# The last expert step's down projection reordered by columns in a decoder layer with 32 experts

## The reference, cut to what matters

```python
def expert_block(args):                 # xb: the tokens of one expert, e: its number
    xb, e = args
    return (jax.nn.silu(xb @ w1[e]) * (xb @ w3[e])) @ w2[e]
...
out = out.at[row_tok].add(yr * row_w[:, None])     # weighted, back to the token's row
...
x = x + hier_moe(rms_norm(x, norm_moe), ...)
return rms_norm(x, final_norm)
```

## Time and profile before

| | us |
|---|---|
| median of 3 runs | 675.01 (674.87 to 675.44) |
| the profiled execution | 675.29 |
| its span | 673.5 |
| PE busy | 511.5 |
| DVE, ACT, POOL busy | 204.5, 145.5, 14.9 |
| DMA moved | 244.21 MB, mean 363 GB/s |

### The profile page before, as it was taken

How to read it: one execution, slowest core, us unless ns; L and a number is a source line. 1 busy time by engine, 2 the same in 40 slices (tenths; PEclk the granted TensorE clock), 3 DMA queues, 4 the chain that set the end, 5 groups by cost and what they waited for, 6 DMA issues and landing times.

```text
span 673.5 us, 8778 instructions
## 1 busy us (share of the span) xinstructions
PE 511.5 (76%) x3804; PEld 322.7 (48%) x3804; DVE 204.5 (30%) x378; ACT 145.5 (22%) x252; POOL 14.9 (2%) x31
## 2 busy tenths in 40 slices
PE   8999999999999997967744846774374667348475
PEld 7999998999999742422311411231141123114121
DVE  4899565588857431100000100000010000001002
ACT  5764545354635411000000000000000000000002
POOL 1200010001001000000000000000000000000001
PEclk9999999999999988997857988786797778679788
DMA  8999236908679999999999999999999999999994
GB/s 290 386 325 326 90 126 198 372 4 300 224 279 387 417 366 431 427 427 427 430 424 431 424 431 424 432 423 429 428 427 429 425 430 427 428 426 429 425 410 168
DMA packets 46041, 244.21 MB, mean 363 GB/s; under 512 B 5968, under 2 KB 15664, under 8 KB 34224
## 3 DMA queue, kind: packets, MB, share of 16 engines
q1 hardware_dynamic: 46000, 243.62, 89.4%
HBM read 242.53 MB, written 4.22 MB: 366 GB/s over the span
## 4 chain that ended last, share of the span: by engine, by line
PE 53%; DMA 44%; DVE 1%; ACT 1%; issue 0%; SPq 0%; POOL 0%; POOLq 0%
PE ps L713 16%; DMA slots_late<-in_w 13%; PE ps L1077 11%; DMA slots_own<-in_w 9%; DMA attn_data<-in_w 7%; PE ps L736 7%; PE ps L1082 6%; DMA slot_spare<-in_w 5%; DMA slot_last<-in_w 5%; DMA slot_mixed<-in_w 4%; PE ps L691 1%; DMA slots_own<-in_w_in 1%; PE ps L837 1%; PE ps L866 1%; PE ps L1187 1%; PE ps L951 1%
## 5 line engine op out<-in xcount | busy, mean ns | idle before, releaser
L1077 PE MATMUL ps<-slots_late,x_sb 128*32 128x512 f32 x320 | 88.2, 697 | 36.6 <-DMA slots_late<-in_w 14.7
L1077 PE MATMUL ps<-slot_spare,x_sb 128*32 128x512 f32 x128 | 60.8, 675 | 13.7 <-DMA attn_data<-in_w 13.7
L1077 PE MATMUL ps<-attn_data,x_sb 128*32 128x512 f32 x160 | 61.9, 701 | 10.7 <-DMA slots_own<-in_w 10.7
L1820 DVE TENSOR_TENSOR slot_extra<-ps,slot_extra 128x512 f32<-128x512 f32 x8 | 5.5, 692 | 212.2 <-ACT slot_extra L1443 212.2
L439 DVE TENSOR_TENSOR w_low<-slots_own,w_high 128x2048 fp32r<-128x2048 f32 (+1 forms) x32 | 64.7, 2021 | 16.8 <-ACT w_high L1251 16.5
L1440 ACT ACTIVATE slot_extra<-ps 128x256 f32<-128x256 f32 x8 | 3.1, 384 | 299.7 <-PE ps L1145 299.7
L1077 PE MATMUL ps<-slots_own,x_sb 128*32 128x512 f32 x240 | 56.7, 664 | 8.8 <-DMA slot_last<-in_w 3.6
L1082 PE MATMUL ps<-slots_own,slot_extra 128*32 128x512 f32 x192 | 50.1, 723 | 16.1 <-DMA slots_late<-in_w 8.0
L1082 PE MATMUL ps<-attn_data,slot_extra 128*32 128x512 f32 x112 | 46.4, 749 | 16.4 <-DMA slots_own<-in_w 16.4
L1251 ACT ACTIVATE w_high<-slots_own 128x2048 fp32r<-128x2048 f32 (+1 forms) x32 | 54.3, 1697 | 19.5 <-PE ps L736 10.8
L713 PE MATMUL ps<-h_high,w_high 128*128 128x256 f32 x224 | 55.4, 288 | 0.0
(11 more groups left out here) (262 smaller groups left out, 868.5 us busy)
## 6 DMA issues: line engine op xcount, KB each, us to landing
slots_own<-in_w SPq DMA_DIRECT2D x27, 2048.0 KB, 31.4
slots_late<-in_w SPq DMA_DIRECT2D x23, 2048.0 KB, 35.0
attn_data<-in_w SPq DMA_DIRECT2D x16, 2048.0 KB, 34.3
slot_last<-in_w SPq DMA_DIRECT2D x9, 2048.0 KB, 35.9
slots_own<-in_w_in SPq DMA_DIRECT2D x8, 2048.0 KB, 10.9
slot_spare<-in_w SPq DMA_DIRECT2D x8, 2048.0 KB, 34.7
slot_mixed<-in_w SPq DMA_DIRECT2D x7, 2048.0 KB, 34.7
slots_own<-in_w_out SPq DMA_DIRECT2D x2, 2048.0 KB, 9.7
```

Of the source, the lines that this page charges most:

```text
L1077: return pe.matmul(ps[SLOTS * e:SLOTS * e + SLOTS, 4 + matrix, :], xeT[:, k, SLOTS * e:SLOTS * e + SLOTS], w, start=(k == 0), stop=(k == K ...
L1820: dve.tensor_tensor(act_sb, ps[:, 5, :].rearrange("p (q f) -> p f q", f=FC), silu_sb.rearrange("p (f q) -> p f q", f=FC), ALU.mult).then_i ...
```

## The change

The diff replaces the tail of the last step. Loads: unit 10's slot now gets depths 2 and 3 of the left columns as two transfers of 1 MB, unit 11's slot depth 2 of the right columns (1 MB) and depth 3 of the right columns in two transfers of 0.5 MB (256 columns each). PE: the right half is computed as two quarters of 256 columns in banks 5 and 6; after the left half is complete, PE waits for ACT's copy of it and does both left scatters, and only then turns to depths 2 and 3 of the right half. DVE copies the right half in two quarters, and the right scatters are done by quarters.

```diff
--- before.py
+++ after.py
@@ -61,6 +61,9 @@
 SLOT = 4096
 SLICE = SLOT // SHARE
 MOE_CHUNKS = 12
+TAIL_LOADS = {10: [(0, 512, 2, 0, 0), (2048, 512, 3, 0, None)],
+              11: [(0, 512, 2, 512, 1), (2048, 256, 3, 512, 2), (3072, 256, 3, 768, None)]}
+TAIL_BANKS = [(4, 0, 512), (5, 512, 256), (6, 768, 256)]
 UNROLL = 2
 TURNS = STEPS // UNROLL
 TURN_CHUNKS = UNROLL * MOE_CHUNKS
@@ -351,7 +354,9 @@
         summed, again_done, fsq, frstd_set, out_written = (
             sem("summed"), sem("again_done"), sem("fsq"), sem("frstd_set"), sem("out_written"))
         left_weighted, left_set = sem("left_weighted"), sem("left_set")
-        var_left_set, last_half_in = sem("var_left_set"), sem("last_half_in")
+        var_left_set = sem("var_left_set")
+        tail_in = [sem(f"tail_in{i}") for i in range(3)]
+        y_mid_done, y_mid_copied = sem("y_mid_done"), sem("y_mid_copied")
         out_set = [sem(f"out_set{t}") for t in range(TT)]
         dve_step, pool_step = sem("dve_step"), sem("pool_step")
         sel_made, moved = sem("sel_made"), sem("moved")
@@ -536,14 +541,12 @@
                     e = step * SHARE + 2 * (j - 8)
                     sp.dma_start(ring[s].rearrange("p (e n) -> p e n", e=2),
                                  expert_weights[2][:, e:e + 2, 0:2 * SLICE]).then_inc(slot_in[s], 16)
-                elif step == STEPS - 1 and j == 10:
-                    load_slice(2, step * SHARE, 2, SLICE, ring[s], slot_in[s])
-                elif step == STEPS - 1 and j == 11:
-                    for c in range(2):
-                        n = 3 * SLICE + 512 * c
-                        sp.dma_start(ring[s].rearrange("p (e c n) -> p c e n", e=SHARE, c=2)[:, c],
-                                     expert_weights[2][:, step * SHARE:(step + 1) * SHARE,
-                                                       n:n + 512]).then_inc(last_half_in if c else slot_in[s], 16)
+                elif step == STEPS - 1 and j in (10, 11):
+                    for at, width, f, c0, signal in TAIL_LOADS[j]:
+                        signal = slot_in[s] if signal is None else tail_in[signal]
+                        src = expert_weights[2][:, step * SHARE:(step + 1) * SHARE, f * D + c0:f * D + c0 + width]
+                        sp.dma_start(ring[s][:, at:at + SHARE * width].rearrange("p (e n) -> p e n", e=SHARE),
+                                     src).then_inc(signal, 16)
                 else:
                     load_unit(j // SHARE, step * SHARE + j % SHARE, s, slot_in[s])
 
@@ -1152,24 +1155,59 @@
                 m.then_inc(actT_done, 1)
                 pe.wait_ge(actT_copied, it + 2)
                 if slices_out:
+
+                    def tail_matmul(piece, f, e, w):
+
+                        bank, _, width = TAIL_BANKS[piece]
+                        return pe.matmul(ps[SLOTS * e:SLOTS * e + SLOTS, bank, 0:width],
+                                         actT[:, f, SLOTS * e:SLOTS * e + SLOTS], w,
+                                         start=(f == 0), stop=(f == FC - 1), skip_group_check=True)
+
+                    def tail_load(j, i):
+
+                        at, width, f, c0, _ = TAIL_LOADS[j][i]
+                        s = unit_landed((STEPS - 1) * MOE_CHUNKS + j)[0]
+                        w = ring[s][:, at:at + SHARE * width].rearrange("p (e n) -> p e n", e=SHARE)
+                        for piece, (_, first, n) in enumerate(TAIL_BANKS):
+                            if c0 <= first < c0 + width:
+                                for e in range(SHARE):
+                                    m = tail_matmul(piece, f, e, w[:, e, first - c0:first - c0 + n])
+                        return m
+
+                    def scatter(t, piece):
+
+                        bank, c0, width = TAIL_BANKS[piece]
+                        return pe.matmul(ps[:, 2 * t + c0 // 512, c0 % 512:c0 % 512 + width],
+                                         selwT[:, t * P:(t + 1) * P], y_sb[:, c0:c0 + width],
+                                         start=False, stop=True, skip_group_check=True)
+
                     w = [unit(8 + i).rearrange("p (e f n) -> p e f n", e=2, f=2) for i in range(2)]
                     for f in range(2):
-                        for c in range(2):
+                        for piece, (_, c0, width) in enumerate(TAIL_BANKS):
                             for e in range(SHARE):
-                                m = down_matmul(c, f, e, w[e // 2][:, e % 2, f, 512 * c:512 * c + 512])
+                                m = tail_matmul(piece, f, e, w[e // 2][:, e % 2, f, c0:c0 + width])
                     m.then_inc(chunk_used, 2)
-                    w = unit(10).rearrange("p (e n) -> p e n", e=SHARE)
-                    for c in range(2):
-                        for e in range(SHARE):
-                            m = down_matmul(c, 2, e, w[:, e, 512 * c:512 * c + 512])
-                    m.then_inc(chunk_used, 1)
-                    w = unit(11).rearrange("p (e n) -> p e n", e=SHARE)
-                    for c in range(2):
-                        if c:
-                            pe.wait_ge(last_half_in, 16)
-                        for e in range(SHARE):
-                            m = down_matmul(c, 3, e, w[:, e, 512 * c:512 * c + 512])
-                        m.then_inc((y_left_done, chunk_used)[c], 1)
+                    pe.wait_ge(tail_in[0], 16)
+                    tail_load(10, 0)
+                    unit(10)
+                    tail_load(10, 1).then_inc(y_left_done, 1)
+                    pe.wait_ge(selwT_copied, it + 2)
+                    pe.wait_ge(y_copied_a, it + 2)
+                    for t in range(TT):
+                        scatter(t, 0).then_inc(summed, 1)
+                    pe.wait_ge(tail_in[1], 16)
+                    tail_load(11, 0).then_inc(chunk_used, 1)
+                    pe.wait_ge(tail_in[2], 16)
+                    tail_load(11, 1).then_inc(y_mid_done, 1)
+                    unit(11)
+                    tail_load(11, 2).then_inc(chunk_used, 1)
+                    pe.wait_ge(y_mid_copied, 1)
+                    scatter(0, 1)
+                    pe.wait_ge(y_copied_v, it + 2)
+                    scatter(0, 2).then_inc(summed, 1)
+                    scatter(1, 1)
+                    scatter(1, 2).then_inc(added, 1)
+                    return
                 else:
                     w = [unit(8 + e).rearrange("p (f n) -> p f n", f=FC) for e in range(SHARE)]
                     for c in range(2):
@@ -1186,8 +1224,6 @@
                     for t in range(TT):
                         m = pe.matmul(ps[:, 2 * t + c, :], selwT[:, t * P:(t + 1) * P], y_sb[:, 512 * c:512 * c + 512],
                                       start=False, stop=True, skip_group_check=True)
-                        if slices_out and c + t < 2:
-                            m.then_inc(summed, 1)
                 m.then_inc(added, 1)
 
             for signal in (added, actT_done, selwT_done):
@@ -1786,7 +1822,7 @@
 
             slots = const[:, K_SLOT:K_SLOT + SLOTS].unsqueeze(1).unsqueeze(1).to_broadcast([P, TT, SHARE, SLOTS])
 
-            def expert_step(it, experts, r, first=False):
+            def expert_step(it, experts, r, first=False, last=False):
                 if first:
                     dve.wait_ge(rank_done, 1)
                 else:
@@ -1821,6 +1857,13 @@
                                   silu_sb.rearrange("p (f q) -> p f q", f=FC), ALU.mult).then_inc(act_set, 1)
                 dve.wait_ge(actT_done, it + 2)
                 dve.tensor_copy(actT.rearrange("p f s -> p (f s)"), ps[:, 6, :]).then_inc(actT_copied, 1)
+                if last:
+                    dve.wait_ge(y_mid_done, 1)
+                    dve.wait_ge(added, it + 1)
+                    dve.tensor_copy(y_sb[:, 512:768], ps[:, 5, 0:256]).then_inc(y_mid_copied, 1)
+                    dve.wait_ge(chunk_used, it * MOE_CHUNKS + MOE_CHUNKS)
+                    dve.tensor_copy(y_sb[:, 768:1024], ps[:, 6, 0:256]).then_inc(y_copied_v, 1)
+                    return
                 dve.wait_ge(chunk_used, it * MOE_CHUNKS + MOE_CHUNKS)
                 dve.wait_ge(added, it + 1)
                 dve.tensor_copy(y_sb[:, 512:1024], ps[:, 5, :]).then_inc(y_copied_v, 1)
@@ -1829,7 +1872,7 @@
                 dve.sem_inc(signal, 1)
             dve.sem_inc(xe_copied, 2)
             for it in range(STEPS):
-                expert_step(it, slice(it * SHARE, it * SHARE + SHARE), 0, first=(it == 0))
+                expert_step(it, slice(it * SHARE, it * SHARE + SHARE), 0, first=(it == 0), last=(it == STEPS - 1))
             dve.wait_ge(most_set, 1)
             fullest = dve.value_load(most_i[0:1, 0:1], min_val=0, max_val=T)
             with dve.If(fullest > SLOTS):
```

## The result

The changed kernel takes 676.21 us, the kernel before 674.83 (medians of 22 runs each): ratio 1.0022, 95% interval 1.0015 to 1.0029. It is slower by about 0.2%; that is small, but the interval leaves out no change. (A ratio here is not the quotient of the two medians; the two differ by up to 0.001.) The forecast was 675.0 with 674.1 to 676.0, so the median lies outside. The profiled execution took 675.88 with a span of 674.1.

What follows compares the result with a forecast made beforehand. The present end was read as hanging on the last load's landing, with 1.6 us of PE slack; after the change PE would set it. 675.01 - 0.5 (earlier squares) + 0.5 (mean clock) = 675.0 us, range 674.1 to 676.0.

Steps and rivals of the forecast that it cites:

- both right squares start 0.5 us earlier: ACT's squares at the end: start 0.5 us earlier, still 0.86 apart, with POOL, DVE and SP following unchanged.
- the sum: Whole kernel: median 675.01, less 0.5 for earlier squares, plus 0.5 for the mean clock, gives 675.0 us.
- PE and not the last load set the end: Last quarter of the right half: its data land at 662.6, 1.3 us early, so PE's work sets the end.
- The sum of PE's terms: PE from 654.53: 1.85 us of waiting goes; 0.9 ACT's copy, 0.3 DVE's, 0.25 switches and starts come in.
- Short passes: PE's 256-column passes in the right half: 0.215 us each, bound 0.25.
- ACT's copy: Between PE's left passes and left scatters: PE idle 0.9 us, to 660.6, waiting for the copy.
- the cut loads: Last weight transfers, cut into smaller pieces: last landing at 662.6, 663.0 at most.
- the gains' landing: Load of the gains behind the weights: lands near 664.0, before DVE wants it.
- DVE's weightings: DVE's two left weightings run from about 665.6 to 667.1, covered by 0.4 us before the inverse root at 667.5.
- The slower rival, late loads: Last 0.5 MB: cut transfers land late; whole gain gone at 664.4, 678.2 us if landing at 667.6; chance 8%.
- The mean-clock term: PE's restart at half clock in the last step: mean clock starts the down matmuls 0.55 us later, longest 1.05.

Runs made afterwards that it cites:

- a_nobranch_warm: Changed kernel without PE's fallback branch, plus 14 matmuls on old data in the wait ahead of the last step's w3 matmuls: 674.28 us, ratio 0.9994.
- a_same: The changed kernel again, unchanged, as a control: ratio 1.0013 against the kernel before.
- a_nobranch: Changed kernel with PE's fallback for fuller experts (its last branch and body) left out: 673.76 us, ratio 0.9987 against the kernel before.
- a_else: Changed kernel with PE's last step put into both arms of its branch, so the jump comes near 612 us: 674.21 us, ratio 0.9994.
- a_mid: Changed kernel with PE's branch moved into the wait ahead of the last step's w3 matmuls, near 628 us: 674.62 us, ratio 1.0001.
- a_later: Changed kernel with one PE wait ahead of its last branch, until its last scatter is done: ratio 1.0014 against the kernel before.
- b_nobranch: Kernel before with PE's fallback for fuller experts (its last branch and body) left out: 674.35 us, ratio 0.9989.
- b_else: Kernel before with PE's last step put into both arms of its branch: 676.90 us, ratio 1.0032, 7 launches only.
- b_mid: Kernel before with PE's branch moved into the wait ahead of the last step's w3 matmuls: 675.76 us, ratio 1.0006.
- a_else_leftlate: As a_else, with the two left scatters moved behind the last quarter's down matmuls: 675.20 us, ratio 1.0007 against the kernel before.
- before: The kernel before the change, unaltered: 674.83 us, median of 22 runs.
- b_late: Kernel before with one PE wait ahead of its last branch, until the second left scatter is done: 676.29 us, ratio 1.0016.
- b_later: Kernel before with one PE wait ahead of its last branch, until PE's last scatter is done: ratio 1.0024.

## Why the prediction was wrong

**The step that failed** is the sentence that both right squares start 0.5 us earlier "and POOL, DVE and SP follow them unchanged". They did, to the issue of the output (1.07 us earlier in the profile); the DMA engines behind them did not. The last piece landed 4.6 us after its issue in place of 2.6, and the output as a whole took 1.65 us more, over three times the gain of 0.5. Put into the sum, 675.0 + 1.65 is 676.65, against the 676.21 measured. The output was costed as a fixed tail, and the one instruction packet at its edge was not looked for, though the trace of before had it, over just as the output began. What is late next was asked only up to the last compute instruction.

**Right, point by point.** PE and not the last load set the end: the chain and `a_nobranch_warm` show it. The sum of PE's terms: from the first down matmul to the right square 11.28 us, and 11.28 again in the profiles of `a_same`, `a_nobranch`, `a_else`, `a_mid` and `a_later`; the forecast was 0.5 below 11.76. Short passes cost 0.215, ACT's copy left PE idle for 0.81, the cut loads landed on time (the last at 662.47, forecast 662.6), the gains' landing at 663.7 (664.0), and DVE's weightings stayed covered. The slower rival, late loads, did not happen; that the time came out on its side is luck, as it was output and not weights that came late.

**The clock.** The mean-clock term was 0.5 us. In this profile the mean clock of the 6 us after the restart was 0.75, higher than in any of the six of the earlier trace rows:

```profile
641.90:647.90 6.00, 5.99 (x44) 1.84 (x48) 0.00 (x0) 0.00 (x0) 0.00 (x0) 0.75 1.00 416
```

In `a_nobranch` the rise came 5.3 us after the restart in place of 3.0 here, and the down matmuls began 13.18 us after it in place of 12.03: half the difference, as the step said. The Trainium skill's rule that this transition moves from run to run (TensorE: Matmul & The Clock Gate, Part 1) agrees with these rises. They lie further apart, 2.3 us, than the 500 ns either way that the page gives. Of the 0.59 us by which the down matmuls began earlier in the changed kernel's profile, 0.38 is an earlier restart (641.91 against 642.29) and 0.21 the clock. But the term's size is not confirmed by medians: without the branch the changed kernel stands 1.25 us below the kernel before, where the sum gives 0. Part of the difference, 0.7, the kernel before gains too when its branch goes. `a_nobranch` against `b_nobranch`, with no fetch in either, is 0.6 us by the medians and 0.0002 by the ratios, with intervals that all but coincide, so a net of 0 as forecast is not refuted.

**What is left open:** whether removing the branch gains the kernel before more than the 0.2 that its profile shows; why one fetch of 0.93 us makes an engine 1.5 to 2.1 late; why the moved jump does not help the kernel before; and why some launches of the changed kernel reach 678 to 680. A version that keeps all work and is clearly faster than the kernel before was not found; `a_else` is the nearest.

## What to carry to other kernels

When a chain is shortened near the end of a program, look at what else is on the DMA engines while the output goes out: a body jumped over at the end makes its engine fetch instructions (two packets of 16 KB here), and the output waits behind them on one of 16 DMA engines. Try such a jump where its engine and the loads have slack, and look at the landings of the last transfers and at the time: here the move helped the changed kernel (1.0022 to 0.9994) and not the kernel before. And count the work that an engine has left when its awaited data land, before taking those data for the bound.

## What the runs showed of the hardware that was not expected

A jump over the fallback took PE's sequencer 3.3 to 3.9 us at the end of the program, where the loads were over. Near 612 and 628 us, under full loads, it took 6.0 to 6.9 us; there the arm jumped over also holds PE's last step or a part of it, so the two causes are not told apart. One such view, of `a_else`:

```profile
L1250 PEldq COMPARE_BRANCH  x1: 6246/6246/6246, 611.4 to 611.4; - x1
```

The granted clock can fall inside the last stage when PE waits between loads: in `b_else`, `b_mid` and `b_nobranch` it did so behind 661 us, and cost 1.5 to 3.1 us each by the first right square's distance from the last landing (5.4 to 7.0 in place of 3.9); in `a_else_leftlate` it fell at 660.3. In `before`, `b_late` and `b_later`, with the same order of PE's work, it did not. In none of the six profiles of the changed order with the left scatters in their place, and no extra matmuls, did it fall there. Whether the order protects against it was not tested by itself.
